# Attention plus retrieved experts on one Trainium2 core: 192 gathered tokens, and the score and value passes run as one behind a lead of 48 blocks

## The chip, the cores and the metric

The kernel runs on one core of a Trainium2 chip. The metric is the device time in microseconds (us), the median of several runs. The core has TensorE (PE: matmuls; its weight loads are shown as PEld), VectorE (DVE), ScalarE (ACT), GpSimd (POOL) and SyncE (SP), which only issues DMAs. Every engine works through its own list of instructions in order and waits on semaphores.

## The reference

One layer of a model: a mixer (sliding-window attention beside an mLSTM), which the change leaves alone, and then a PEER layer of retrieved experts. The second part, for 512 tokens `h` of 1024 numbers, in full precision:

```
q = (ht @ w_q).reshape(T, 8, 2, 128)
s1, s2 = q[:, :, 0] . keys1, q[:, :, 1] . keys2          # 128 keys each
v1, i1 = top_k(s1, 16); v2, i2 = top_k(s2, 16)
top, pos = top_k(v1[..., :, None] + v2[..., None, :], 16)
eidx = (i1 * 128 + i2) at pos                            # 8 x 16 experts of 16384
gate = softmax(top)
act = gelu(u[eidx] . ht) * gate
y = sum over the 128 chosen experts of act * v[eidx]
```

## The kernel before

The 16384 experts lie in 128 blocks of 128 rows of `peer_u` and `peer_v` (1024 numbers each). The first 128 tokens are served by **gathering**: per token and choice one row of `peer_u` is fetched with an indirect DMA (one DMA is a row for each of the 128 tokens, 512 KB), VectorE takes its dot product with the token (L1442), and later the row of `peer_v` is added with its coefficient (L1692); that is 128 gathers of each table. The other 384 tokens are served **densely**: all 128 blocks are multiplied with all these tokens, and a table of gates, zero for experts that a token did not choose, picks out the right ones.

Full precision is had from the reduced-precision matmul format by splitting an operand into a high part (a ScalarE copy) and a low part (VectorE: value minus high part) and adding three products: high by high, high by low, low by high.

Three stages matter here, each a program block of its own that all engines enter and leave together. `query_block` (until about 480 us) makes queries and key scores, and the 16 best of each half. `expert_block` goes over the blocks of `peer_u`: eight transposes turn a block (L1385), ScalarE makes `uH` from PSUM (L1342), VectorE makes `uL` (L1436), 24 matmuls with 384 columns give the scores (L1397, L1400), ScalarE applies Gelu (L1351), and SP stores the result in a table in DRAM. Beside the first 48 of these blocks VectorE ranks the candidates of the four tiles of 128 tokens. Then come 64 blocks that also carry a gate step each: for six tokens VectorE makes two one-hot matrices per token (L1523, L1524), TensorE multiplies them (L1408; one full-precision product is two MATMUL records), and ScalarE copies the 128 x 128 gates of each token into `stage` (L1361), from where SP stores them in DRAM. Sixteen blocks without gates end the stage. `value_block` goes over the blocks of `peer_v`: it loads scores and gates back, VectorE multiplies them into `a` (L1678), both `a` and the block are split (L1651, L1653, L1684, L1687), and 18 matmuls with 512 columns add into six PSUM banks (L1731). Last come the norm (squares at L1661) and the output.

The order is written out by hand: in the lead VectorE's `beside` counts elements worked and puts a `low` where enough have passed.

## Time and profile before

| | |
|---|---|
| median of 3 runs | 1782.9 us (1781.66 to 1788.79) |
| profiled execution, its own time | 1785.9 us |
| its span | 1784.2 us |
| TensorE busy | 94% of the span |
| VectorE, ScalarE busy | 78%, 37% |
| mean granted TensorE clock | 0.968 of full |
| moved by DMA | 426.72 MB |

Busy time is what an engine spent in instructions; matmuls are pipelined, so their durations overlap, and the pace of TensorE is read from starts or from counts of records in a stretch. The span runs from the first to the last instruction; the run's own time is 1.7 us longer.

### The profile page before, as it was taken

Reading aid. Unit: us, or ns where it says so; the run is one execution under the profiler, and the core shown is the slowest. Engines: PE = TensorE matmul, PEld = TensorE weight load, DVE = VectorE, ACT = ScalarE, POOL = GpSimd, SP = SyncE. Lnnn points to the kernel's source line nnn. Section 1 sums busy time; section 2 is a strip of 40 time slices with the busy share of each in tenths; the row PEclk is TensorE's granted clock in tenths of the full one; section 3 lists DMA queues with packets and bytes.
Section 4 is the critical chain, followed back from the end, with each engine's and each line's share of the span. In section 5 each row is a group of like instructions: output and inputs, shape, how many; then the busy total and the mean of one; then the engine's idle time right before and its main releaser. Section 6 shows DMA issues by size and latency. Waiting matters only on the chain. (4 is left out here: it accounts for less than half of the span.)

```text
span 1784.2 us, 26835 instructions
## 1 busy us (share of the span) xinstructions
PE 1670.8 (94%) x8654; PEld 1424.9 (80%) x8654; DVE 1385.7 (78%) x3141; ACT 662.0 (37%) x946; POOL 379.3 (21%) x327
## 2 busy tenths in 40 slices
PE   3999889599699999899999999998999999999996
PEld 2445444378599999899999999997888888888885
DVE  5967556659979997598888888753988888888885
ACT  1102241422144434355555555523333333333332
POOL 1000000034002111132222222221522222232220
PEclk8998999899899999999999999998999999999998
DMA  9562030231146555498888888885999999999981
GB/s 357 181 236 107 1 141 1 58 107 48 60 136 240 187 203 181 146 327 287 303 287 301 290 298 294 298 321 196 407 369 355 354 350 355 356 354 348 359 301 67
DMA packets 178084, 426.72 MB, mean 239 GB/s; under 512 B 14489, under 2 KB 91377, under 8 KB 178033
## 3 DMA queue, kind: packets, MB, share of 16 engines
q1 hardware_dynamic: 131760, 249.68, 39.3%
q0 software_dynamic: 45264, 174.08, 27.9%
q10 hardware_dynamic: 1008, 2.38, 0.4%
q8 instruction: 20, 0.33, 0.1%
q14 instruction: 32, 0.25, 0.0%
HBM read 373.66 MB, written 52.43 MB: 239 GB/s over the span
## 5 line engine op out<-in xcount | busy, mean ns | idle before, releaser
L1397 PE MATMUL S_ps<-hH,uH 128*128 128x384 f32 x1024 | 357.3, 349 | 0.0
L1397 PE MATMUL S_ps<-hL,uH 128*128 128x384 f32 x1024 | 346.3, 338 | 0.0
L1322 POOL DMA_INDIRECT hT<-in_peer_u,eidx x128 | 162.9, 1272 | 543.3 <-DVE dots L1442 475.6
L1651 ACT ACTIVATE vH<-ring 128x1024 fp32r<-128x1024 f32 x128 | 135.8, 1061 | 312.2 <-PE y_ps L1731 309.2
L1731 PE MATMUL y_ps<-vH,aH 128*128 128x512 f32 x768 | 237.7, 391 | 2.1 <-DVE aL L1687 2.1
L1731 PE MATMUL y_ps<-vH,aL 128*128 128x512 f32 x768 | 237.4, 390 | 0.0
L1731 PE MATMUL y_ps<-vL,aH 128*128 128x512 f32 x768 | 237.4, 390 | 0.0
L1436 DVE TENSOR_TENSOR uL<-uT_ps,uH 128x1024 fp32r<-128x1024 f32 x128 | 156.3, 1221 | 101.6 <-ACT uH L1342 97.5
L1684 DVE TENSOR_TENSOR vL<-ring,vH 128x1024 fp32r<-128x1024 f32 x128 | 156.8, 1225 | 85.0 <-ACT vH L1651 85.0
L1621 POOL DMA_INDIRECT hT<-in_peer_v,eidx x128 | 143.6, 1122 | 342.6 <-DVE y L1692 336.4
L1400 PE MATMUL S_ps<-hH,uL 128*128 128x384 f32 x1024 | 201.1, 338 | 2.2 <-DVE uL L1436 2.2
L1397 PEld LDWEIGHTS S_ps<-hL,uH 128*128 128x128 f32 x1024 | 193.2, 189 | 0.0
L1397 PEld LDWEIGHTS S_ps<-hH,uH 128*128 128x128 f32 x1024 | 193.2, 189 | 0.0
L1400 PEld LDWEIGHTS S_ps<-hH,uL 128*128 128x128 f32 x1024 | 182.2, 188 | 2.5 <-DVE uL L1436 2.5
L1731 PEld LDWEIGHTS y_ps<-vH,aH 128*128 128x128 f32 x768 | 144.8, 189 | 32.9 <-DVE aL L1687 2.8
L1731 PEld LDWEIGHTS y_ps<-vL,aH 128*128 128x128 f32 x768 | 144.7, 188 | 30.2
L1731 PEld LDWEIGHTS y_ps<-vH,aL 128*128 128x128 f32 x768 | 144.7, 188 | 30.2
L1351 ACT ACTIVATE act_out<-S_ps 128x384 f32<-128x384 f32 x128 | 62.8, 491 | 282.0 <-PE S_ps L1400 281.6
L1692 DVE SCALAR_TENSOR_TENSOR y<-hT,coef,y 128x1024 f32<-128x1024 f32 x128 | 163.6, 1278 | 0.9 <-DMA hT<-in_peer_v,eidx 0.9
L1442 DVE CUSTOM_DVE_ANT_0 hT<-hT,h_rows 128x1024 f32<-128x1024 f32 x128 | 152.7, 1215 | 2.7 <-DMA hT<-in_peer_u,eidx 2.7
L1385 PE MATMUL uT_ps<-ident,ring 128*128 128x128 f32 x1024 | 135.0, 276 | 15.8 <-DMA ring<-in_peer_u 15.8
L1342 ACT ACTIVATE uH<-uT_ps 128x1024 fp32r<-128x1024 f32 x128 | 133.9, 1046 | 33.0 <-PE uT_ps L1385 32.7
(277 smaller groups left out, 2387.4 us busy)
## 6 DMA issues: line engine op xcount, KB each, us to landing
ring<-in_peer_u SPq DMA_DIRECT2D x128, 512.0 KB, 5.8
ring<-in_peer_v SPq DMA_DIRECT2D x128, 512.0 KB, 5.6
gelu_table<-act_out SPq DMA_DIRECT2D x128, 192.0 KB, 4.2
gate_table<-stage SPq DMA_DIRECT2D x32, 768.0 KB, 7.5
s_in<-gelu_table SPq DMA_DIRECT2D x128, 192.0 KB, 5.5
...
```

What stands on the lines that cost most here:

```text
L1322: pool.indirect_dma_start(u_rows[:, k % RING, :], None, A["peer_u"][0], bass.IndirectOffsetOnAxis(eidx[:, k:k + 1], 0)).then_inc(rows_in[k ...
L1342: func(uH[:, b, :], uT_ps[:, b, :], ACT.Copy).then_inc(u_high, 1)
L1385: last = tr(uT_ps[:, b, c * P:(c + 1) * P], ub[:, r, c * P:(c + 1) * P], ident[:])
L1397: mm(S_ps[:, b, 0:TD], uH[:, b, c * P:(c + 1) * P], h[:, c, P:T], start=(c == 0 and h is hH), stop=False)
L1400: last = mm(S_ps[:, b, 0:TD], uL[:, b, c * P:(c + 1) * P], hH[:, c, P:T], start=False, stop=(c == DC - 1))
L1436: v.tensor_tensor(uL[:, b, :], uT_ps[:, b, :], uH[:, b, :].bitcast(F32), ALU.subtract).then_inc(u_low, 1)
L1442: v.tensor_tensor_reduce(out=u_rows[:, q, :], in0=u_rows[:, q, :], in1=h_rows[:], scale=1.0, scalar=0.0, op0=ALU.mult, op1=ALU.add, accum_ ...
L1621: pool.indirect_dma_start(v_rows[:, k % RING, :], None, A["peer_v"][0], bass.IndirectOffsetOnAxis(eidx[:, k:k + 1], 0)).then_inc(rows_in[k ...
L1651: func(vH[:, q, :], vb[:, q, :], ACT.Copy).then_inc(v_hi, 1)
L1684: v.tensor_tensor(vL[:, q, :], vb[:, q, :], vH[:, q, :].bitcast(F32), ALU.subtract).then_inc(v_lo, 1)
L1692: v.scalar_tensor_tensor(out=y0[:, q % 2, :], in0=v_rows[:, q, :], scalar=coef[:, bass.ds(n, 1)], in1=y0[:, q % 2, :], op0=ALU.mult, op1=A ...
L1731: last = mm(y_ps[:, t, h, :], x[:, q, t * P:(t + 1) * P], w[:, q, h * 512:(h + 1) * 512], start=False, stop=False)
```

## The change

- 192 tokens are gathered instead of 128. The extra 64 need only half a gather's rows per choice, so two choices share one DMA: 64 more gathers of each table, 384 in all. 320 tokens are left for the dense way.
- Six gather buffers instead of four.
- `expert_block` and `value_block` become one `peer_block`. Its first part, the **lead**, has turns 0 to 47: scores of 48 blocks, stored to DRAM, and within them all gate steps (80 steps of four tokens, in turns 19 to 47: 16, 32 and 32 steps for the three token tiles, at one or two, three or four, and four per turn). From turn 48 on each turn does the scores of one block and the values of a block scored two turns before, without DRAM between (80 turns); the 48 lead blocks get their values at the end, in 48 turns and two that drain.
- In the lead the low part is made without VectorE: TensorE adds minus the high part to the block in PSUM (two matmuls, `lead_less`), and ScalarE copies what is left (`lead_low`).
- Of a gate step's one-hot matrices VectorE makes the first of all four tokens in one instruction and the second of two; ScalarE makes the second of the other two, by Abs and Relu (`gate_rows`). The gate product is written to PSUM with a step of four elements, and ScalarE stages four tokens at once (`stage_gates`).
- The ranking works on one tile at a time and hands each on: softmax in `settle` (VectorE), turned by TensorE, copied back in `choice_turned`, at turns 9, 18, 29 and 39.
- In the fused part the block is turned and split in halves. High and low parts of `a` lie interleaved; for the first 64 dense tokens one weight load of both serves, so a value takes 16 matmuls instead of 18, and a fold at the end adds them up. There is one slot for the split value block while scores run, and two after.
- The gather turns are planned ahead: 56 rows in the lead, 284 in the 80 fused turns (three or four each), 44 in 44 of the last ones.
- `query_block` also transposes the 64 extra tokens (eight transposes, two copies).

The core of the diff:

```
-GT = 6
+NA, NB = P, 64
+T0 = NA + NB
+TD = T - T0
+KB = K * NB // P
+GT = 4
-TB = 2 * GT
+TB = 20
-BG = 16
-GP = BG // 4
+BG = 8
+NHOT = 4
+RING = 4
+PE_BLOCK, PE_STEP = 4.8, 0.92
-RING = 4
-TAIL = NBLK - LEAD - GSTEPS
-LOW_EVERY = 2900
-DOTS_LEAD = 20
-DOTS_AFTER = GSTEPS + 8
+SEL_AT = {0: 9, 1: 18, 2: 29, 3: 39}
+ROWS_LEAD, ROWS_TAIL = (40, 16), 44
+NF = NBLK - LEAD
+END = LEAD + 2 + NBLK
+ORDER = list(range(LEAD, NBLK)) + list(range(LEAD))
+TILES = [0, 2, 3, 1]
+RG = 6
+NROWS = 2 * (K + KB)
+STEPS_OF = {1: NB // GT, 2: P // GT, 3: P // GT}
+EIDX_B_AT = RG
...
+def gate_steps():
+    steps, m = [[] for _ in range(LEAD)], 0
+    ends = {1: SEL_AT[2], 2: SEL_AT[3], 3: LEAD - 1}
+    for t in (1, 2, 3):
+        for it, n in spread(STEPS_OF[t], range(SEL_AT[t] + 1, ends[t] + 1)).items():
+            steps[it] = list(range(m, m + n))
+            m += n
+    return steps
...
+                if j == EIDX_B_AT:
+                    pool.wait_ge(eidx_ready, 2)
+                    pool.dma_start(eidx[NB:P, K:K + KB], chosen_u[0:NB, 0, KB:K]).then_inc(eidx_b_in, 16)
...
+            def lead_high(n):
+                act.wait_ge(u_turned, n + 1)
+                if n >= 2:
+                    act.wait_ge(u_done, n - 1)
+                func(H[:, n % 2, :], uT_of(n % 2), ACT.Copy).then_inc(u_high, 1)
+            def lead_low(n):
+                act.wait_ge(u_less, n + 1)
+                func(L[:, n % 2, :], uT_of(n % 2), ACT.Copy).then_inc(u_low, 1)
...
+            def gate_rows(m):
+                b, q = m % NHOT, m % 2
+                act.wait_ge(selT_done, 2 * tile_of(m))
+                if m >= NHOT:
+                    act.wait_ge(g_full, m - NHOT + 1)
+                for k in range(GT - 2, GT):
+                    d = GT * m + k
+                    ins = func(away[:, q, k - GT + 2, :], iota[:], ACT.Abs, bias=negT[:, 0, d:d + 1])
+                ins.then_inc(away_done, 1)
+                act.wait_ge(away_done, m + 1)
+                for k in range(GT - 2, GT):
+                    d = GT * m + k
+                    ins = func(onehot[:, b, k, 1, :], away[:, q, k - GT + 2, :], ACT.Relu, scale=negT[:, 1, d:d + 1], bias=selT[:, 2, d:d + 1])
+                ins.then_inc(hot_act, 1)
+            def stage_gates(m):
+                q, t0 = m // (TB // GT), GT * (m % (TB // GT))
+                act.wait_ge(g_full, m + 1)
+                if t0 == 0 and q >= 2:
+                    act.wait_ge(g_stored[q % 2], 16 * (q // 2))
+                func(stage[:, q % 2, :, t0:t0 + GT], ps[:, 6 + m % 2, :].rearrange("p (i t) -> p i t", t=GT), ACT.Copy).then_inc(g_staged, 1)
...
+            for it in range(LEAD):
+                if it + 1 < LEAD:
+                    lead_high(it + 1)
+                    lead_low(it + 1)
+                gelu(it, 4 + it % 2)
+                for t in range(NT):
+                    if it == SEL_AT[t] - 1:
+                        act.wait_ge(top_ready, t + 1)
+                        func(top[:, t, :, :], top[:, t, :, :], ACT.Exp).then_inc(gate_exp, 1)
+                for m in STEPS[it]:
+                    stage_gates(m)
+                if it + 1 < LEAD:
+                    for m in STEPS[it + 1]:
+                        gate_rows(m)
...
+            for n in range(LEAD, END):
+                w = n - LEAD - 1
+                if LEAD < n <= NBLK:
+                    gelu(n - 1, 6 + (n - 1) % 2)
+                if n < NBLK:
+                    act.wait_ge(half_turned, n - LEAD + 1)
+                    act.wait_ge(u_done, n)
+                    func(H[:, 0, 0:512], ps[:, 6 + n % 2, :], ACT.Copy).then_inc(ua_high, 1)
+                if 0 <= w < NBLK:
+                    act.wait_ge(a_ready, w + 1)
+                    if w >= 2:
+                        act.wait_ge(v_done, w - 1)
+                    func(aHL[:, w % 2, :, 0], a[:, w % 2, :], ACT.Copy).then_inc(a_hi, 1)
+                if n < NBLK:
+                    act.wait_ge(u_turned, n + 1)
+                    func(H[:, 0, 512:D], ps[:, 7 - n % 2, :], ACT.Copy).then_inc(ub_high, 1)
+                if 0 <= w < NBLK:
+                    act.wait_ge(v_in[w % RING], 16 * (w // RING + 1))
+                    wait_slot(act, w)
+                    func(H[:, slot_of(w), :], vb[:, w % RING, :], ACT.Copy).then_inc(v_hi, 1)
...
+            def lead_less(n):
+                pe.wait_ge(u_high, n + 1)
+                for i in range(2):
+                    last = mm(ps[:, 2 * (n % 2) + i, :], minus_one[:], H[:, n % 2, i * 512:(i + 1) * 512],
+                              start=False, stop=True, skip_group_check=True)
+                last.then_inc(u_less, 1)
+            def scores_high(bank, b):
                 for c in range(DC):
                     for h in (hH, hL):
+                        mm(ps[:, bank, 0:TD], H[:, b, c * P:(c + 1) * P], h[:, c, T0:T], start=(c == 0 and h is hH), stop=False)
+            def scores_low(bank, b):
                 for c in range(DC):
+                    last = mm(ps[:, bank, 0:TD], L[:, b, c * P:(c + 1) * P], hH[:, c, T0:T], start=False, stop=(c == DC - 1))
                 last.then_inc(u_done, 1)
...
+            def gates(m):
+                pe.wait_ge(hot_dve, m + 1)
+                pe.wait_ge(hot_act, m + 1)
+                if m >= 2:
+                    pe.wait_ge(g_staged, m - 1)
+                for k in range(GT):
+                    last = mm(ps[:, 6 + m % 2, :].rearrange("p (i t) -> p t i", t=GT)[:, k, :], onehot[:, m % NHOT, k, 0, :],
+                              onehot[:, m % NHOT, k, 1, :], start=True, stop=True)
+                last.then_inc(g_full, 1)
...
+            for it in range(LEAD):
+                if it + 1 < LEAD:
+                    lead_turn(it + 1)
+                pe.wait_ge(u_high, it + 1)
+                if it >= 2:
+                    pe.wait_ge(s_ready, it - 1)
+                scores_high(4 + it % 2, it % 2)
+                if it + 1 < LEAD:
+                    lead_less(it + 1)
+                pe.wait_ge(u_low, it + 1)
+                scores_low(4 + it % 2, it % 2)
+                for m in STEPS[it]:
+                    gates(m)
...
+            def value(w, part):
+                s, b, first, final = slot_of(w), w % 2, w == 0, w == NBLK - 1
+                aH, aL = aHL[:, b, :, 0], aHL[:, b, :, 1]
+                both = aHL[:, b, 0:NB, :].rearrange("p t i -> p (t i)")
+                if part == 0:
+                    pe.wait_ge(v_hi, w + 1)
...
+                            mm(y_bank(g, h), aH[:, NB + g * P:NB + (g + 1) * P], H[:, s, h * 512:(h + 1) * 512], start=first, stop=False)
+                else:
...
+                    pe.wait_ge(v_lo, w + 1)
+                    for g in range(2):
+                        for h in range(2):
+                            mm(y_bank(g, h), aH[:, NB + g * P:NB + (g + 1) * P], L[:, s, h * 512:(h + 1) * 512], start=False, stop=final)
+                    for h in range(2):
+                        last = mm(y_bank(2, h), both, L[:, s, h * 512:(h + 1) * 512], start=False, stop=final)
+                    last.then_inc(v_done, 1)
...
+            for n in range(LEAD, END):
+                w = n - LEAD - 2
...
+                if n < NBLK:
+                    pe.wait_ge(u_in[n % RING], 16 * (n // RING + 1))
+                    turn(n, 0)
+                if w >= 0:
+                    value(w, 0)
+                if n < NBLK:
+                    if n > LEAD:
+                        pe.wait_ge(s_ready, n)
+                    turn(n, 1)
+                if w >= 0:
+                    value(w, 1)
+                if n < NBLK:
+                    pe.wait_ge(ua_high, n - LEAD + 1)
+                    pe.wait_ge(ub_high, n - LEAD + 1)
+                    pe.wait_ge(ua_low, n - LEAD + 1)
+                    scores_high(6 + n % 2, 0)
+                    pe.wait_ge(ub_low, n - LEAD + 1)
+                    scores_low(6 + n % 2, 0)
...
+            def hot_rows(m):
+                b, d0 = m % NHOT, GT * m
+                if m >= NHOT:
+                    dve.wait_ge(g_full, m - NHOT + 1)
+                v.tensor_tensor(onehot[:, b, :, 0, :], iota[:].unsqueeze(1).broadcast_to([P, GT, P]),
+                                selT[:, 0, d0:d0 + GT].unsqueeze(2).broadcast_to([P, GT, P]), ALU.is_equal)
+                for k in range(GT - 2):
+                    d = d0 + k
+                    ins = v.tensor_scalar(onehot[:, b, k, 1, :], iota[:], selT[:, 1, d:d + 1], selT[:, 2, d:d + 1], ALU.is_equal, ALU.mult)
+                ins.then_inc(hot_dve, 1)
+            clock, due, blk = 0.0, 0.0, 0
...
+            for n in range(LEAD, END):
+                w = n - LEAD - 1
+                left = ROWS_AT[n]
+                if n < NBLK:
+                    dve.wait_ge(ua_high, n - LEAD + 1)
+                    v.tensor_tensor(L[:, 0, 0:512], ps[:, 6 + n % 2, :], H[:, 0, 0:512].bitcast(F32), ALU.subtract).then_inc(ua_low, 1)
+                if 0 <= w < NBLK:
+                    if w < NF:
+                        dve.wait_ge(s_ready, LEAD + w + 1)
+                        src = act_out[:, (LEAD + w) % 2, :]
+                    else:
+                        dve.wait_ge(s_loaded[w % RING], 16 * ((w - NF) // RING + 1))
+                        src = s_in[:, w % RING, :]
+                    g = (w // BG) % 2
+                    dve.wait_ge(g_in[g], 16 * (w // (2 * BG) + 1))
+                    if w >= 2:
+                        dve.wait_ge(a_hi, w - 1)
+                    v.tensor_tensor(a[:, w % 2, :].rearrange("p (q t) -> p q t", t=TB), src.rearrange("p (q t) -> p q t", t=TB),
+                                    gbuf[:, g, :, w % BG, :], ALU.mult).then_inc(a_ready, 1)
+                if n < NBLK and left > 3:
+                    take_row()
+                    left -= 1
+                if n < NBLK:
+                    dve.wait_ge(ub_high, n - LEAD + 1)
+                    v.tensor_tensor(L[:, 0, 512:D], ps[:, 7 - n % 2, :], H[:, 0, 512:D].bitcast(F32), ALU.subtract).then_inc(ub_low, 1)
+                if left > 1:
+                    take_row()
+                    left -= 1
+                if 0 <= w < NBLK:
+                    dve.wait_ge(a_hi, w + 1)
+                    v.tensor_tensor(aHL[:, w % 2, :, 1], a[:, w % 2, :], aHL[:, w % 2, :, 0].bitcast(F32), ALU.subtract).then_inc(a_lo, 1)
+                if left > 1:
+                    take_row()
+                    left -= 1
+                if 0 <= w < NBLK:
+                    dve.wait_ge(v_hi, w + 1)
+                    s = slot_of(w)
+                    v.tensor_tensor(L[:, s, :], vb[:, w % RING, :], H[:, s, :].bitcast(F32), ALU.subtract).then_inc(v_lo, 1)
+                for _ in range(left):
+                    take_row()
+            assert rows_taken == NROWS
```

## Rows read from the trace of the kernel before

**Rows 1.** The page, part 1: busy us, share, instructions.
```profile
PE 1670.8 (94%) x8654; PEld 1424.9 (80%) x8654; DVE 1385.7 (78%) x3141; ACT 662.0 (37%) x946; POOL 379.3 (21%) x327
```

**Rows 2.** Stretches: us, busy per engine (x records), granted clock, DMA share, GB/s.
```profile
500.00:700.00 200.00, 200.00 (x1260) 198.72 (x1258) 177.40 (x374) 84.31 (x100) 33.46 (x20) 1.00 0.57 192
800.00:1100.00 300.00, 300.00 (x2051) 300.00 (x2050) 266.32 (x744) 164.85 (x208) 82.34 (x70) 1.00 0.86 296
1300.00:1700.00 400.00, 400.00 (x1766) 331.22 (x1766) 329.29 (x393) 144.39 (x196) 114.31 (x122) 1.00 0.96 354
1244.00:1260.00 16.00, 16.00 (x66) 13.03 (x65) 16.00 (x21) 7.60 (x10) 12.39 (x7) 0.90 1.03 403
718.00:740.00 22.00, 17.59 (x100) 16.80 (x99) 8.94 (x22) 6.79 (x9) 0.00 (x0) 0.84 0.38 122
```

**Rows 3.** Timeline of PE: first turn; one lead block.
```profile
481.84 3.68 PE L1385 MATMUL uT_ps<-ident,ring 128*128 128x128 f32 x16 [15.84 <-DMA ring<-in_peer_u]
...
562.45 0.34 PE L1397 MATMUL S_ps<-hH,uH 128*128 128x384 f32 x1
...
564.73 0.34 PE L1397 MATMUL S_ps<-hL,uH 128*128 128x384 f32 x1
```

**Rows 4.** Groups of ScalarE: busy us, mean ns of one.
```profile
L1651 ACT ACTIVATE vH<-ring 128x1024 fp32r<-128x1024 f32 x128 | 135.8, 1061 | 312.2 <-PE y_ps L1731 309.2 <-PEq L1718 2.8 <-DMA ring<-in_peer_v 0.2
...
L1342 ACT ACTIVATE uH<-uT_ps 128x1024 fp32r<-128x1024 f32 x128 | 133.9, 1046 | 33.0 <-PE uT_ps L1385 32.7
...
L1361 ACT ACTIVATE stage<-G_ps 128x384 f32<-128x384 f32 x128 | 101.1, 898 | 39.4 <-PE G_ps L1408 39.4
...
L1653 ACT ACTIVATE aH<-a 128x384 fp32r<-128x384 f32 x128 | 65.0, 508 | 16.9 <-DVE a L1678 16.9
L1351 ACT ACTIVATE act_out<-S_ps 128x384 f32<-128x384 f32 x128 | 62.8, 491 | 282.0 <-PE S_ps L1400 281.6
...
L1351 ACT ACT_TABLE_LOAD x28 | 35.9, 1283 | 43.9 <-PE S_ps L1400 43.9
...
L1134 ACT ACTIVATE peer_qT<-query_psum 128x512 f32<-128x512 f32 x16 | 9.6, 598 | 73.3 <-PE query_psum L1180 73.3
```

**Rows 5.** Timeline of ScalarE: small activations with a bias column.
```profile
257.84 0.39 ACT L651 ACTIVATE decay<-x_sb,gcol 128x128 f32<-128x128 f32 x1
258.13 0.39 ACT L649 ACTIVATE decay<-x_sb,gcol 128x128 f32<-128x128 f32 x1
```

**Rows 6.** Groups of VectorE: busy us, mean ns of one.
```profile
L1692 DVE SCALAR_TENSOR_TENSOR y<-hT,coef,y 128x1024 f32<-128x1024 f32 x128 | 163.6, 1278 | 0.9 <-DMA hT<-in_peer_v,eidx 0.9
...
L1442 DVE CUSTOM_DVE_ANT_0 hT<-hT,h_rows 128x1024 f32<-128x1024 f32 x128 | 152.7, 1215 | 2.7 <-DMA hT<-in_peer_u,eidx 2.7
...
L1523 DVE TENSOR_SCALAR onehot<-iota,selT 128x128 f32<-128x128 f32 x384 | 110.4, 288 | 22.6 <-PE G_ps L1408 20.3
```

**Rows 7.** Timeline of VectorE: one value block.
```profile
1400.62 1.23 DVE L1684 TENSOR_TENSOR vL<-ring,vH 128x1024 fp32r<-128x1024 f32 x1 [0.72 <-ACT vH L1651]
1401.77 0.55 DVE L1687 TENSOR_TENSOR aL<-a,aH 128x384 fp32r<-128x384 f32 x1
1402.23 1.28 DVE L1692 SCALAR_TENSOR_TENSOR y<-hT,coef,y 128x1024 f32<-128x1024 f32 x1
1403.43 0.55 DVE L1678 TENSOR_TENSOR a<-s_in,s_all 128x384 f32<-128x384 f32 x1
```

**Rows 8.** VectorE from 479 to 701: all, L1436, L1442; one wait.
```profile
479.00:701.00 222.00, 196.12 (x462) 0.98 0.57 192
...
479.00:701.00 222.00, 52.62 (x43) 0.98 0.57 192
...
479.00:701.00 222.00, 19.57 (x32) 0.98 0.57 192
...
DVE uL L1436 <- ACT uH L1342: 20.2, 14, 3.5
```

**Rows 9.** The chain in order of time: start, us, what.
```profile
1241.52 525.17 PE y_ps L1731 x2304
```

732 lines of the change are left out of this document (339 added, 393 removed).

## The prediction

> **What bounds the kernel now.** I read the page's busy times first [rows 1]: TensorE is at 94%, VectorE at 78%, ScalarE at 37%. An average says little over stages, so the stretches came next [rows 2]. From 500 to 1700 TensorE is busy throughout but for two gaps, at full clock. Records give its pace. Lead: 32 per block, 1260 in 200 us, 5.08 us a block. Gate blocks: 44 per block, 2051 in 300 us, 6.44 us. Value blocks: 525.17 us for 128 [rows 9], 4.10 us. The reader is to see that VectorE, at 89% beside the first two and 82% in the third, is close behind, and that DMA moves 354 GB/s in the values at a share of 0.96. So fewer TensorE columns pay one for one, as long as the other engines keep up at the new pace.
>
> **Unit prices.** 384-column matmuls start 0.1754 us apart (13 steps from 562.45 to 564.73 [rows 3]); 24 take 4.21 of the 5.08, which leaves 0.87 for eight transposes. 512 columns: 400 us for 1766 [rows 2], 0.2265. The line through both gives 0.150 for 320 columns, an estimate. One one-hot product: (6.44 - 5.08)/6 = 0.226. VectorE, start to start [rows 7]: split of 1024 1.15, of 384 0.46, row added 1.20; so 0.60 for 512 and 0.39 for 320. A dot is 1.215 long and starts about 0.07 early on the next, 1.145 [rows 6]. ScalarE [rows 4]: 1024 long 1.05, 512 from PSUM 0.60, 384 0.49; a small one with a bias column 0.39 long, the next 0.30 later [rows 5]; a table load 1.28.
>
> **Part by part.**
>
> Query stage: eight more transposes and two copies, +1.5. TensorE begins the lead at 481.8 [rows 3], then at 483.3.
>
> Lead on TensorE alone: a block is 24 x 0.150 + 0.87 + 2 x 0.2265 = 4.92; a gate step 4 x 0.226 = 0.90. 48 x 4.92 + 80 x 0.90 = 308, so it could end at 791. VectorE does not stop it in total: the ranking cost it 222 - 43 splits x 1.15 - 16 dots x 1.145 - 20 of waiting [rows 8] = 134; 80 gate steps at 0.59 + 2 x 0.26 = 1.1 (the one-hot of 512 elements by the 512 price, the other two by L1523) are 88; 56 dots 64; hand-overs 8: 294.
>
> ScalarE does. Its order in a turn is: high part of the next block, low part, Gelu, staging of this turn's gates, one-hots for the next turn. A step's one-hots are two Abs, a wait for their own result, two Relu: 0.30 + 0.39 + 0.05 + 0.30 + 0.30, about 1.3. Nothing of this overlaps TensorE's half of the loop: `lead_less` of the next block needs the high part, which stands behind the one-hots; these stand behind the staging of the last gate; that stands behind the scores' low products. Queued behind ScalarE's wait are the Gelu, the stores and the next Abs. The loop with k steps now and k' next is 1.2 (low products) + 0.9k + 0.8 (last result, staging) + 1.3k' + 1.0 (high) + 0.65 (two matmuls and their result) = 3.65 + 0.9k + 1.3k'. At k = 3 that is 10.3 against 7.6 of TensorE, at k = 4 12.5 against 8.5. Turns 0 to 18 have no steps: 19 x 4.92, 3 for two switches to Exp and back (two loads and 0.3 each, partly covered), 1.5 for the slow first turn: 98. Turns 19 to 29: 11 x 3.65 + 16 x 2.2 = 75, and about 10 for the first hand-over (Exp, `settle`, transposes, copy, one-hots, gates, each after the other): 85. Turns 30 to 47: 18 x 3.65 + 64 x 2.2 = 206, and 5 for the hand-over at 39: 211. Lead 394, ending at 877. Bounds: if the Abs and Relu were hidden, the lead is TensorE's 308 and the 20 of hand-overs, switches and slow start, ending at 811, 66 less; with staging at the 0.90 of L1361, whose writes are strided as these are in part, +12 to +25. I take contiguous runs of four as free.
>
> Staging and gate product: the product goes to PSUM with a step of four elements. No row shows such a write. The line above makes 0.0004 us of a column, 0.051 of 128 columns, and the records of L1408 stand 0.113 apart (0.226 for two), so over half of each is slack for the write. I take nothing; four times the time would add 0.9 a step, 72.
> The Trainium skill (SBUF — State Buffer, Door 1: The DMA port swizzle) says that any non-contiguous access to PSUM slows matmuls significantly. By that rule the sum would be some 70 higher; by the row it is not.
>
> Hand-over to the fused part: scores of turns 48 and 49 need no values, 2 x 4.47 + 1 = 10. The first `a` waits for the last gate store, then two gate groups of 1.3 MB, behind four value blocks; 4.7 MB with the store at 403 GB/s [rows 2] and some 4 of latency is 16 after the lead's end, where VectorE blocks at 7. The stall is 9, and 1 more for the clock: a stop of 9.5 cost 0.84 over 22 before [rows 2]. +10.
>
> Fused turns, 78: 3.60 + 0.87 + 16 x 0.2265 = 8.09, 631. VectorE: two halves 1.2, `a` and its low part 0.78, value split 1.15, 3.55 rows x 1.15 to 1.20: 7.2 to 7.4, below 8.09. ScalarE 3.2. The single value slot is free at 4.5 of a turn, high part to 5.6, low part to 7.0, needed at 9.9 of the same count: hidden. DMA: 0.52 for each block, 0.16 of gates, 3.55 x 0.52 of rows = 3.07 MB a turn, 380 GB/s. Before, 403 GB/s ran for 16 us [rows 2], so 7.6 us a turn: hidden, with 6% to spare. I add 4.
>
> Last 50 turns: TensorE needs 16 x 0.2265 = 3.62. But VectorE does `a`, its low part, the value split, then the row; ScalarE makes the value's high part only after the high part of `a`. With `a` of the next turn behind the row on VectorE this closes a loop: split 1.15, row 1.20, `a` 0.48 + 0.03, ScalarE 0.38 to its next, value high 1.06 + 0.03 [rows 4, 7] = 4.33. 44 x 4.33 + 6 x 3.62 = 212, 31 more than TensorE's own.
>
> End: before 17.5 from the last value matmul (1766.7 to 1784.2). Six closing matmuls go (1.4), two copies and two more squares come (2.5): 18.6.
>
> Sum: 877 + 10 + 10 + 631 + 212 + 18.6 + 4 = 1762.6 of span, against 1784.2: 21.6 less. The profiled run was 3 above the median, so the forecast is 1782.9 - 22 = 1761 us. Of some 147 us that the cut in TensorE's work would give, 86 go to ScalarE's loop and hand-overs in the lead, 31 to the loop at the end.
>
> **The rivals.**
> A, the lead is TensorE's and VectorE's: ScalarE's one-hots hide. For it: ScalarE is at 37%, and in a turn of k = 4 it is busy only 9.5 us. Against: the order above. Then 877 becomes 811: 1695.
> Where the Abs and Relu stand in one table set with Gelu they cost no load, which no row shows; the Trainium skill (ScalarE: Activation LUTs, Table sets: the hidden batching unit) says that every set has both.
> B, the other side: DMA bounds the fused turns. For it: 354 GB/s at a share of 0.96 [rows 2] may be the ceiling, not the demand; then a turn is 3.07/0.354 = 8.68 and the gathers, whose buffers come free as VectorE takes rows, come late: +47 less the 4, 1804. It makes the kernel slower from 31 us on, a turn of 8.5, that is a rate under 362 GB/s. Against: 403 GB/s with both queues full.
> C, the strided gate products: +72, 1833. Against: the slack above.
> D, the end runs at TensorE's pace, 3.62: -31, 1730. Then ScalarE gets `a` early enough.
> E, the stops of 3 to 4 us in each late lead turn let the clock fall; half of TensorE's 5 us in the loop doubled over 18 turns is +45, 1806. From 800 on before, TensorE never stopped, so no row excludes it.
>
> **How the numbers follow.** Chances: forecast 0.40 (own range 1735 to 1790), A 0.20, B 0.16, C 0.06, D 0.08, E 0.10. 1761 is the forecast's own time. From 1690, which takes in A, to 1815, which takes in B and E, all but C and the far ends stand: 0.8. Half a per cent is 9 us, about what a measurement can tell: faster is under 1774, slower over 1792. Faster: A, D, and 0.28 of the forecast, 0.56. Slower: B, C, E less 0.06, and 0.02, 0.28. Same 0.16.
>
> **What would show it.** Lead: L1385 to the end of the gate products 394 us; ScalarE's high part of the late turns waits for nothing but its own one-hots, and `lead_less` waits 3 to 4 us for it in each of turns 30 to 47; granted clock 1.00. VectorE some 100 us idle there. Fused: 8.1 us a turn, rows never late by DMA. End: 4.3 us a turn, ScalarE waiting for `a`. It would be wrong if ScalarE's small activations overlap more than 0.30 apart, if gathers land later than 9 us, or if the gate records are longer than 0.113 apart.

## The result and the profile after

The changed kernel takes 1812.6 us (median of four runs, 1810.1 to 1814.1) beside 1784.5 for the kernel before on the same chip: ratio 1.014, 95% interval 1.013 to 1.016. It is slower by 1.4%, and the interval lies clear of 1. The forecast was 1761. The profiled execution has a span of 1808.2, where the working summed to 1762.6, so 45.6 us are to be found.

The page's busy times of the changed kernel, to be read against [rows 1]: TensorE has 73 us less to do, and yet the span is 24 longer.

```profile
PE 1598.1 (88%) x8370; PEld 1331.0 (74%) x8370; DVE 1384.5 (77%) x2859; ACT 725.2 (40%) x1307; POOL 500.1 (28%) x424
```

Its stretches, with the columns of [rows 2] (busy time per engine, granted clock, DMA share, GB/s):

```profile
500.00:700.00 200.00, 174.65 (x1197) 167.69 (x1196) 174.35 (x461) 130.95 (x221) 51.35 (x37) 0.97 0.69 225
700.00:800.00 100.00, 75.75 (x443) 72.23 (x442) 37.67 (x89) 68.05 (x142) 12.25 (x10) 0.79 0.51 160
800.00:900.00 100.00, 68.70 (x423) 65.49 (x423) 48.82 (x114) 70.79 (x156) 18.35 (x14) 0.84 0.60 187
900.00:1000.00 100.00, 80.86 (x468) 74.90 (x469) 64.33 (x111) 36.87 (x69) 34.91 (x30) 0.87 0.87 314
1000.00:1500.00 500.00, 500.00 (x2959) 457.17 (x2959) 457.47 (x637) 188.88 (x309) 251.88 (x220) 1.00 0.99 380
1600.00:1700.00 100.00, 93.34 (x380) 71.38 (x380) 76.56 (x93) 33.24 (x47) 19.85 (x21) 1.00 0.92 318
```

The reader is to see three kinds of stretch. From 1000 to 1500, the fused part, TensorE never stops and its clock is 1.00. From 1600 on it stops for 7% of the time, at full clock. From 700 to 900 no engine is full: TensorE 76 and 69%, VectorE 38 and 49%, ScalarE 68 and 71%. That is what a loop of hand-overs looks like; and there the granted clock is 0.79 and 0.84. A busy share is also higher at half clock, because the same work takes longer.

One late lead turn of four gate steps, ScalarE's timeline (start, duration, line, out<-in, count, idle time before and what ended it):

```profile
817.60 0.69 ACT L1462 ACTIVATE s_all<-iota,negT 128x128 f32<-128x128 f32 x2
818.32 0.88 ACT L1467 ACTIVATE s_all<-s_all,selT,negT 128x128 f32<-128x128 f32 x2
819.11 0.68 ACT L1462 ACTIVATE s_all<-iota,negT 128x128 f32<-128x128 f32 x2
...
822.83 0.88 ACT L1467 ACTIVATE s_all<-s_all,selT,negT 128x128 f32<-128x128 f32 x2
823.62 1.00 ACT L1438 ACTIVATE hi_slots<-peer_psum 128x1024 fp32r<-128x1024 f32 x1
825.93 1.02 ACT L1443 ACTIVATE lo_slots<-peer_psum 128x1024 fp32r<-128x1024 f32 x1 [1.31 <-PE peer_psum L1550]
828.03 0.44 ACT L1451 ACTIVATE s_all<-peer_psum 128x320 f32<-128x320 f32 x1 [1.07 <-PE peer_psum L1561]
828.92 0.60 ACT L1475 ACTIVATE stage<-peer_psum 128x512 f32<-128x512 f32 x1 [0.45 <-PE peer_psum L1570]
...
831.72 0.60 ACT L1475 ACTIVATE stage<-peer_psum 128x512 f32<-128x512 f32 x1 [0.30 <-PE peer_psum L1570]
832.22 0.69 ACT L1462 ACTIVATE s_all<-iota,negT 128x128 f32<-128x128 f32 x2
```

The same turn on TensorE (the sixteen high products, L1557, start at 817.9 and are left out):

```profile
816.91 1.04 PE L1542 MATMUL peer_psum<-ident,ring 128*128 128x128 f32 x8
824.67 1.22 PE L1550 MATMUL peer_psum<-hi_slots,minus_one 128*128 128x512 f32 x2 [4.38 <-ACT hi_slots L1438]
825.69 2.30 PE L1561 MATMUL peer_psum<-hH,lo_slots 128*128 128x320 f32 x8
827.83 3.86 PE L1570 MATMUL peer_psum<-s_all 128*128 128x128 f32 x32
```

Read the two together, from 817.60 to the same point at 832.22, 14.6 us. ScalarE makes four steps' one-hots (6.0 us, 1.51 each), then the high part. TensorE had its transposes at 817 and its high products by 820.3, and stops 4.38 us. When it goes on it is at half clock: two `lead_less` products take 1.22, eight low products 2.30 (1.34 at full clock, below). ScalarE waits for each of them in turn, stages four gates, and starts again. While ScalarE finishes its one-hots and the high part TensorE has nothing to do. Behind that the two answer each other, and only the first stagings run beside gate products.

Turns, from the start of one Gelu to the next: up to 18 mostly 4.86 us each, 19 to 29 7.7 on average (84.3 in all). In turns 30 to 47 those of three steps take 11.3 to 13.4 and those of four 15.2 on average; they alternate between about 14.8 and 15.7, because in every second one part of the gate products is at the lower clock too (32 of them take 5.03 us from 842.43, for 3.86 above). The last gate products end at 919.9, and the transposes of turn 48 start at 920.6.

The hand-over after the lead, VectorE's first `a` and TensorE's first high products after it, from the timeline:

```profile
927.13 0.80 SPq L1363 DMA_DIRECT2D stage<-gate_table  x2
...
940.66 0.49 DVE L1841 TENSOR_TENSOR s_all<-s_all,stage 128x320 f32<-128x320 f32 x1 [12.36 <-DMA stage<-gate_table]
...
941.58 0.57 ACT L1510 ACTIVATE hi_slots<-peer_psum 128x512 fp32r<-128x512 f32 x1
```

```profile
942.25 0.61 PE L1557 MATMUL peer_psum<-hH,hi_slots 128*128 128x320 f32 x1 [14.56 <-ACT hi_slots L1510]
942.65 0.47 PE L1557 MATMUL peer_psum<-hL,hi_slots 128*128 128x320 f32 x1
942.92 0.47 PE L1557 MATMUL peer_psum<-hH,hi_slots 128*128 128x320 f32 x1
```

Products of 320 columns start 0.27 us apart here; in an early lead turn at full clock it is 0.146. The engine had stopped for 14.56 us, and this pace, 1.8 times slower, is that of the lower of the two clock levels, 1.2 of 2.4 GHz. The regular fused turns then run from 948.1, 8.12 us each. The waits of the whole execution (total, times, longest):

```profile
ACT a_hi_lo L1507 <- DVE s_all L1841: 190.5, 85, 13.6
...
DVE s_all L1734 <- PE peer_psum L1570: 110.0, 17, 8.8
...
PE peer_psum L1550 <- ACT hi_slots L1438: 76.4, 25, 4.8
...
ACT lo_slots L1443 <- PE peer_psum L1550: 56.0, 44, 3.1
```

The largest waits of ScalarE and VectorE are not the loss: VectorE's 110 us are idle time beside the loop. The row that counts is the third, TensorE's 76.4 us in 25 stops: from turn 30 on there are 17, of 2.9 to 4.8 us each.

### The profile page after: what moved, and what is told of

Its sections match the earlier page's. It is cut to its first block, busy times and chain, and to the rows that moved or that the text cites. A ratio compares the mean times of both kernels' runs of the same rounds, so it can differ in the third digit from the quotient of the medians.

```text
span 1808.2 us, 23463 instructions
## 1 busy us (share of the span) xinstructions
PE 1598.1 (88%) x8370; PEld 1331.0 (74%) x8370; DVE 1384.5 (77%) x2859; ACT 725.2 (40%) x1307; POOL 500.1 (28%) x424
## 4 chain that ended last, share of the span: by engine, by line
PE 47%; ACT 10%; DVE 8%; issue 7%; DMA 1%; another core or an unknown queue 0%; SPq 0%; DVEq 0%; ACTq 0%
PE peer_psum L1557 12%; PE peer_psum L1561 8%; PE peer_psum L1570 5%; PE peer_psum L1618 4%; PE peer_psum L1629 4%; PE peer_psum L1625 4%; PE peer_psum L1605 4%; DVE s_all L1706 3%; ACT hi_slots L1514 3%; ACT s_all L1462 3%; ACT s_all L1467 2%; PE peer_psum L1622 2%; PE peer_psum L1631 2%; PE peer_psum L1550 2%; ACT hi_slots L1438 1%
## 5 line engine op out<-in xcount | busy, mean ns | idle before, releaser
L1557 PE MATMUL peer_psum<-hH,hi_slots 128*128 128x320 f32 x1024 | 309.0, 315 | 15.6 <-ACT hi_slots L1510 14.6
L1557 PE MATMUL peer_psum<-hL,hi_slots 128*128 128x320 f32 x1024 | 304.6, 311 | 0.0
L1557 PEld LDWEIGHTS peer_psum<-hH,hi_slots 128*128 128x128 f32 x1024 | 194.7, 190 | 19.5 <-issue 14.8
L1557 PEld LDWEIGHTS peer_psum<-hL,hi_slots 128*128 128x128 f32 x1024 | 194.8, 190 | 3.0
L1561 PE MATMUL peer_psum<-hH,lo_slots 128*128 128x320 f32 x1024 | 187.1, 329 | 0.0
L1561 PEld LDWEIGHTS peer_psum<-hH,lo_slots 128*128 128x128 f32 x1024 | 173.4, 206 | 5.6
L1861 DVE TENSOR_TENSOR lo_slots<-s_all,hi_slots 128x1024 fp32r<-128x1024 f32 x128 | 156.6, 1224 | 21.7 <-ACT hi_slots L1514 21.7
L1618 PE MATMUL peer_psum<-hi_slots,a_hi_lo 128*128 128x512 f32 x512 | 151.4, 417 | 12.3 <-ACT hi_slots L1514 12.3
L1706 DVE SCALAR_TENSOR_TENSOR s_all<-hT,coef,s_all 128x1024 f32<-128x1024 f32 x126 | 161.3, 1280 | 1.0 <-DMA hT<-in_peer_v,eidx 0.9
L1625 PE MATMUL peer_psum<-hi_slots,a_hi_lo 128*128 128x512 f32 x512 | 139.3, 393 | 0.0
L1618 PEld LDWEIGHTS peer_psum<-hi_slots,a_hi_lo 128*128 128x128 f32 x512 | 90.5, 195 | 39.7 <-ACT hi_slots L1514 29.1
L1625 PEld LDWEIGHTS peer_psum<-hi_slots,a_hi_lo 128*128 128x128 f32 x512 | 99.2, 194 | 20.1
L1550 PE MATMUL peer_psum<-hi_slots,minus_one 128*128 128x512 f32 x96 | 40.7, 512 | 76.4 <-ACT hi_slots L1438 76.4
## 6 DMA issues: line engine op xcount, KB each, us to landing
slab<-in_w_mod SPq DMA_DIRECT2D x5, 2048.0 KB, 15.2
```

The costliest lines, as they stand in the source:

```text
L1550: last = mm(ps[:, 2 * (n % 2) + i, :], minus_one[:], H[:, n % 2, i * 512:(i + 1) * 512], start=False, stop=True, skip_group_check=True)
L1557: mm(ps[:, bank, 0:TD], H[:, b, c * P:(c + 1) * P], h[:, c, T0:T], start=(c == 0 and h is hH), stop=False)
L1561: last = mm(ps[:, bank, 0:TD], L[:, b, c * P:(c + 1) * P], hH[:, c, T0:T], start=False, stop=(c == DC - 1))
L1618: mm(y_bank(g, h), aH[:, NB + g * P:NB + (g + 1) * P], H[:, s, h * 512:(h + 1) * 512], start=first, stop=False)
L1625: mm(y_bank(g, h), aL[:, NB + g * P:NB + (g + 1) * P], H[:, s, h * 512:(h + 1) * 512], start=False, stop=False)
L1706: v.scalar_tensor_tensor(out=y0[:, i, :], in0=rows_of(j), scalar=c, in1=y0[:, i, :], op0=ALU.mult, op1=ALU.add).then_inc(row_done, 1)
```

## The experiments

All are edits of the changed kernel. The ratio is to the kernel before on the same chip; 0.01 is 18 us, and the changed kernel's ratio is 1.0143. "Lead" runs from the first transposes to the Gelu of turn 48 in the profiled execution. (The first transposes start anywhere from 476.5 to 485.4 us in these executions, so ends of stretches can't be compared as they stand.) The last column is a lead turn of four steps, the commonest value of turns 41 to 46 or, where they alternate, their mean.

| kernel | median us | ratio, 95% interval | lead us | four steps |
|---|---|---|---|---|
| changed | 1812.6 | 1.0143 (1.0126 to 1.0160) | 448.8 | 15.2 |
| e1_rows_after_high | 1767.2 | 0.9881 (0.9842 to 0.9920) | 401.4 | 13.45 |
| e2_onehots_on_vector | 1722.7 | 0.9633 (0.9597 to 0.9670) | 353.8 | 8.80 |
| e3_clock_kept | 1785.1 | 0.9979 (0.9958 to 1.0000) | 419.3 | 13.18 |
| e4_row_before_low | 1790.0 | 1.0007 (0.9980 to 1.0033) | 442.1 | 15.2 |
| e5_low_by_vector | 1860.8 | 1.0414 (1.0389 to 1.0438) | 496.5 | 16.0 |
| e6_gates_first | 1801.6 | 1.0067 (1.0046 to 1.0089) | 445.4 | 15.2 |
| e7_three_edits | 1692.1 | 0.9468 (0.9444 to 0.9491) | 352.3 | 8.80 |
| e8_planner_price | 1686.0 | 0.9441 (0.9416 to 0.9465) | 347.1 | 8.80 |
| e9_low_behind_rows | 1773.7 | 0.9909 (0.9874 to 0.9945) | 411.3 | 10.5 |
| e10_two_and_two | 1752.4 | 0.9808 (0.9770 to 0.9845) | 389.1 | 11.33 |
| e11_shared_one_hots | 1690.3 | 0.9446 (0.9415 to 0.9477) | 347.6 | 8.80 |

### e1_rows_after_high: the order on ScalarE

```
                 if it + 1 < LEAD:
                     lead_high(it + 1)
+                for m in STEPS[it]:
+                    gate_rows(m)
+                if it + 1 < LEAD:
                     lead_low(it + 1)
...
                     stage_gates(m)
-                if it + 1 < LEAD:
-                    for m in STEPS[it + 1]:
-                        gate_rows(m)
```

> ScalarE's one-hots of a turn are made behind the high part of the next block instead of ahead of it; the work is the same. Loop theory (the high part stands behind the one-hots, and TensorE can do nothing without it): a turn of four steps falls from 15.2 us to ScalarE's own 1.05 + 4 x 1.51 + 1.0 + 0.4 + 1.6 = 10.1 us or a little over, TensorE's stop before `lead_less` goes, and the granted clock stays near 1.00; the lead ends some 80 us sooner, 1725 to 1740 us. Rival, VectorE or the hand-overs set the late turns: no change, within 9 us of 1812. Rival, ScalarE's amount of work and not its order sets the pace: under 20 us saved.

1767 us: 47 less by the ratios, where 72 to 87 were expected. TensorE's stop before `lead_less` is gone, and turns of three steps take 9.4 us. But four steps take 13.45, not 10.1 (the mean of turns 41 to 46 is 12.9), and the clock is 0.95 from 700 to 770 and 0.90 from 770 to 870, not near 1.00. Order is what matters, so both rivals fall; but half of the saving at four steps is missing. TensorE's timeline of this kernel says why:

```profile
812.78 3.04 PE L1570 MATMUL peer_psum<-s_all 128*128 128x128 f32 x16 [3.13 <-ACT stage L1475]
...
819.50 0.62 PE L1550 MATMUL peer_psum<-hi_slots,minus_one 128*128 128x512 f32 x2
819.96 1.34 PE L1561 MATMUL peer_psum<-hH,lo_slots 128*128 128x320 f32 x8
```

The stop has moved to the third gate product: the products have two banks, and ScalarE stages the first only behind all its one-hots, the low part and the Gelu. e10 tests that.

### e10_two_and_two: give the banks back earlier

The edit is shown against e1.

```
                 if it + 1 < LEAD:
                     lead_high(it + 1)
-                for m in STEPS[it]:
+                for m in STEPS[it][:2]:
                     gate_rows(m)
...
+                todo = list(STEPS[it])
+                for i, m in enumerate(STEPS[it][2:]):
+                    gate_rows(m)
+                    for _ in range(2 if i == 0 else 1):
+                        stage_gates(todo.pop(0))
+                for m in todo:
+                    stage_gates(m)
```

> As e1_rows_after_high, but ScalarE makes only the first two steps' one-hots ahead of the low part; those of the third and fourth step alternate with the stagings. Theory for what e1 left (13.45 us at four steps, where ScalarE is busy 10.1): the third gate product needs one of the two gate banks, which ScalarE gives back only behind all its one-hots, the low part and the Gelu, and the next block's transposes stand behind the products. With the banks given back between the one-hots: 11.2 to 12 us at four steps, 9.4 at three as in e1, 10 to 18 us less: 1750 to 1757. Rival, it is something else (the low clock, the one-hots of VectorE): within 5 us of 1767.

1752 us, as expected, 13 under e1 by the ratios. Of turns 41 to 46 three take 11.33, and the others 12.7 to 13.0; the mean is 12.1 for e1's 12.9. TensorE's stop at the third gate product falls from 3.1 to 1.65, with one of 0.80 at the fourth, and from 800 to 857, ahead of the hand-over, the clock is still 0.91. So the bank was a part of e1's rest and not all of it.

### e2_onehots_on_vector: ScalarE's part moved away

```
-                for k in range(GT - 2):
+                for k in range(GT):
                     d = d0 + k
                     ins = v.tensor_scalar(onehot[:, b, k, 1, :], ...)
...
-                pe.wait_ge(hot_act, m + 1)
```
and `gate_rows` is not called.

> All four second one-hots of a step are made by VectorE with its compare-and-multiply; ScalarE's Abs and Relu go. VectorE gets 80 x 2 x 0.26 = 42 us more in the lead. Loop theory: a late turn is TensorE's 8.5 us or VectorE's 8.7; the lead ends about 100 us sooner, 1705 to 1725 us. Rival, VectorE is as close to the bound as ScalarE, because of the ranking: 1750 or more. If the clock's fall had another cause than the stops, it would still show 0.8 from 700 on here.

1722.7 us, inside what was expected: 91 less than the changed kernel. A turn of four steps is 8.80, one of three 7.65. The stretch from 700 to 800, beside the changed kernel's 75.75 and 0.79:

```profile
700.00:800.00 100.00, 97.79 (x740) 95.21 (x738) 91.04 (x253) 56.84 (x81) 23.66 (x19) 1.00 0.88 293
```

TensorE is full and at full clock; VectorE, with 42 us more to do, is at 91%. VectorE takes 0.26 us for the one-hot that costs ScalarE 0.75 (half of 1.51), and it stood idle there. Its timeline in this kernel, the four second one-hots of a step (the next instruction starts at 778.09):

```profile
777.06 1.11 DVE L1734 TENSOR_SCALAR s_all<-iota,selT 128x128 f32<-128x128 f32 x4
```

So the work stood on the wrong engine for this stage of the loop: ScalarE was the less busy engine on the page, and the one that everything waited for.

### e3_clock_kept: what the clock alone costs

```
                 scores_high(4 + it % 2, it % 2)
+                if len(STEPS[it]) >= 3:
+                    for i in range(24):
+                        mm(ps[:, 4 + it % 2, 0:TD], zeros[:], hH[:, i % DC, T0:T], start=False, stop=False)
```

`zeros` is a matrix of zeros, made once, so the products add nothing.

> The order of the lead stays; in turns with three or more gate steps TensorE does 24 more 320-column products with a zero matrix (adding nothing) where it stops, 3.6 us. Theory that the stops cost twice, once as a wait and once by the clock: granted clock 0.95 or more from 700 to 930, `lead_less` and the low products at 0.6 and 1.3 us instead of 1.2 and 2.3, a late turn of 13.3 to 13.7 us, 25 to 35 us less: 1778 to 1787. Rival, the clock costs nothing here because ScalarE alone sets the loop: within 9 us of 1812. Rival, the clock falls for a reason other than the stops: clock as before and the 24 products lengthen nothing or up to 40 us.

More work, and 29 us less by the ratios; the lead is 29.5 shorter. Two rows of stretches and TensorE's timeline of a late turn:

```profile
700.00:800.00 100.00, 94.79 (x693) 92.55 (x692) 44.90 (x107) 78.06 (x163) 14.84 (x12) 1.00 0.58 184
800.00:900.00 100.00, 93.14 (x674) 90.27 (x673) 52.59 (x120) 75.89 (x165) 20.55 (x16) 0.98 0.72 226
```

```profile
823.72 0.72 PE L1552 MATMUL peer_psum<-hi_slots,minus_one 128*128 128x512 f32 x2 [0.85 <-ACT hi_slots L1439]
824.28 1.33 PE L1563 MATMUL peer_psum<-hH,lo_slots 128*128 128x320 f32 x8
```

`lead_less` takes 0.72 for 1.22 and the low products 1.33 for 2.30. The gate products take 3.85 in every turn, where the changed kernel has 3.9 to 4.1 and 5.0 to 5.2 by turns. A turn of four steps is 13.18 and one of three 11.17. That is the loop at full clock. The forecast's formula gives 12.5 and 10.3, and with 1.51 instead of 1.3 for a step's one-hots 13.3 and 10.9.

### e4_row_before_low: the last 50 turns

```
-                if n < NBLK and left > 3:
+                if left > (3 if n < NBLK else 0):
                     take_row()
                     left -= 1
```

> In the last 50 turns VectorE takes its row between `a` and the low part of `a`, not behind the value's low part; the work is the same. Theory of the loop at the end (`a` of the next turn stands behind the row, ScalarE's high value part behind the high part of `a`): the loop shortens by the 1.20 of a row to under TensorE's 3.62, the last 50 turns fall from 208 to 182 to 188 us, 1786 to 1793 in all. Rival, the value blocks' DMA or the wait for the free slot sets the 4.25 us: no change. Rival, TensorE then waits for the low part of `a`, which is now 1.2 late: under 8 us saved.

1790.0 us, 24 less by the ratios, as expected. VectorE's timeline of the changed kernel in this part:

```profile
1660.82 1.28 DVE L1706 SCALAR_TENSOR_TENSOR s_all<-hT,coef,s_all 128x1024 f32<-128x1024 f32 x1
1662.01 0.48 DVE L1841 TENSOR_TENSOR s_all<-s_in,stage 128x320 f32<-128x320 f32 x1
1663.06 0.49 DVE L1854 TENSOR_TENSOR a_hi_lo<-s_all,a_hi_lo 128x320 fp32r<-128x320 f32 x1 [0.56 <-ACT a_hi_lo L1507]
1663.99 1.23 DVE L1861 TENSOR_TENSOR lo_slots<-s_all,hi_slots 128x1024 fp32r<-128x1024 f32 x1 [0.44 <-ACT hi_slots L1514]
```

and of e4:

```profile
1663.14 0.48 DVE L1841 TENSOR_TENSOR s_all<-s_in,stage 128x320 f32<-128x320 f32 x1
1663.54 1.28 DVE L1706 SCALAR_TENSOR_TENSOR s_all<-more_rows,coef,s_all 128x1024 f32<-128x1024 f32 x1
1664.78 0.49 DVE L1854 TENSOR_TENSOR a_hi_lo<-s_all,a_hi_lo 128x320 fp32r<-128x320 f32 x1
```

In the changed kernel VectorE stands idle twice in a turn, each time for ScalarE's answer. With the row put into the first of these gaps the gap is filled, `a` comes sooner, the turn falls from 4.32 to 3.72 us and TensorE is full (100 of the 100 us from 1600 on). The same instructions in another order save 0.6 us a turn.

### e5_low_by_vector and e9_low_behind_rows: the low parts back on VectorE

In both, `lead_less` and ScalarE's `lead_low` are gone, and VectorE subtracts:

```
+            def lead_low(n):
+                dve.wait_ge(u_high, n + 1)
+                if n >= 2:
+                    dve.wait_ge(u_done, n - 1)
+                v.tensor_tensor(L[:, n % 2, :], uT_of(n % 2), H[:, n % 2, :].bitcast(F32), ALU.subtract).then_inc(u_low, 1)
```

> The lead's low parts go back to VectorE, which subtracts the high part from the block in PSUM; TensorE's two products with minus one and ScalarE's copy of the rest go, everything else stays as changed. Loop theory: the high part of the next block is then wanted a turn later, so ScalarE's one-hots are out of the loop and only its own work counts: at four steps 4 x 1.51 + 1.03 + 0.42 + 4 x 0.54 = 9.7 us a turn instead of 15.2. VectorE gets 48 x 1.15 = 55 us more in the lead, at most 350 of the 437. The lead ends 60 to 80 us sooner: 1732 to 1752 us, granted clock 0.95 or more from 700 on. Rival, the low parts were rightly taken off VectorE (the ranking leaves it no room): the turns up to 30 get as much longer as the later ones get shorter, 1790 or more.

1860.8 us, 48 above the changed kernel, where 60 to 80 less were expected. VectorE's timeline (and TensorE's gate products after it):

```profile
851.56 1.22 DVE L1742 TENSOR_TENSOR lo_slots<-peer_psum,hi_slots 128x1024 fp32r<-128x1024 f32 x1 [7.07 <-ACT hi_slots L1438]
852.70 0.68 DVE L1729 TENSOR_TENSOR s_all<-iota,selT 128x512 f32<-128x512 f32 x1
...
853.95 5.47 PE L1568 MATMUL peer_psum<-s_all 128*128 128x128 f32 x32 [6.00 <-DVE s_all L1733]
```

The low part was put ahead of VectorE's own one-hots of the turn. It waits 7.07 us for ScalarE's high part, which stands behind ScalarE's one-hots; VectorE's one-hots stand behind that wait, and TensorE's gates behind those. The loop was not opened, it was led over one engine more. In e9 the low part stands behind VectorE's one-hots:

> As e5_low_by_vector, but VectorE makes the low part of the next block behind its one-hots of the turn, not ahead of them. In e5 the low part waited for ScalarE's high part, which stands behind ScalarE's one-hots, and VectorE's one-hots stood behind that wait: the loop had only moved to VectorE (16 us a turn). Theory that this queue was all of e5's late loss: a turn of four steps falls from 16 to 10.5 to 12 us, VectorE's wait of 7 us before the low part ends no longer ahead of the gates; with turns 0 to 18 at some 6 us as in e5 (VectorE is full there) the lead ends 80 to 100 us sooner than e5's, 1760 to 1785 us, that is 30 to 50 under the changed kernel. Rival, VectorE's low part is late by itself: still 14 us or more a turn, 1830 or more.

1773.7 us, as expected; four steps take 10.5 us in three of turns 41 to 46 and 11.0 to 12.0 in the others, and VectorE's wait is 2.5:

```profile
877.56 1.22 DVE L1742 TENSOR_TENSOR lo_slots<-peer_psum,hi_slots 128x1024 fp32r<-128x1024 f32 x1 [2.53 <-ACT hi_slots L1438]
```

Both kernels pay in the early turns, where VectorE still ranks: turns 1 to 18 take 6.2 and 6.3 us on average against 5.0. From the first transposes to the Gelu of turn 29 e5 takes 219.6 us and e9 217.8, the changed kernel 186.5: the rival of e5's expectation holds there, and it is 33 of the 48 us. In turns 30 to 47 e5 takes 265.7, e9 183.8 and the changed kernel 251.0: there the place in the queue decides. So with the one-hots shared as they are, each of the two places for the low part is the better one in one part of the lead: TensorE and ScalarE while VectorE ranks, VectorE once ScalarE makes one-hots. No run combines them.

### e6_gates_first: the hand-over to the fused part

```
-            for w in range(RING):
-                load_v(w)
             for i in range(2):
                 sp.wait_ge(g_stored[i], 16 * (NTB // 2))
-            for i in range(2):
-                load_g(i)
+            load_g(0)
+            for w in range(RING):
+                load_v(w)
+                if w == 1:
+                    load_g(1)
```

> Between lead and fused part SyncE loads the first group of gates ahead of the value blocks and the second behind two of them, not both behind four. Theory that the first `a` waits for 4.7 MB of which it needs 1.3: its wait on the gates falls from 12.4 us to 3 to 6, the stop of TensorE from 14.6 to 6 to 8, 1803 to 1807 us. Rival, the time is the store of the last gates and a DMA's latency, not what stands ahead: no change, 1812.

1801.6 us, 14 less by the ratios, a little more than the 6 to 10 expected. Waits of e6 from 780 to 960 us:

```profile
PE peer_psum L1558 <- ACT hi_slots L1511: 7.7, 1, 7.7
DVE s_all L1842 <- DMA stage<-gate_table: 5.5, 1, 5.5
```

The wait on the gates falls from 12.4 to 5.5 and TensorE's stop from 14.6 to 7.7, as expected. The turn that holds it, 21.8 us from Gelu to Gelu in the changed kernel, takes 15.0. The traces show these 7 us; the other 7 are not explained, and the intervals of the two ratios leave some 5 us either way.

### e7, e8 and e11: together, and two finer shares

> e2_onehots_on_vector (all one-hots on VectorE), e4_row_before_low (tail) and e6_gates_first (order of loads) together. If the three losses lie in different stages they add: 1722.7 - 22 - 8 = 1693 us, from 1688 to 1700. If e4's saving depended on the pace before it, or the transition's on the DMA traffic, 1700 to 1715.

1692.1 us, as expected. The single savings, 91, 24 and 14, sum to 129; together they give 121 by the ratios. They are losses of different stages and nearly add.

e8 changes one number of e7, `clock += 1.15` to `clock += 1.67`.

> e7 with one number more: the price that VectorE's planner sets for a step's one-hots is 1.67 us instead of 1.15, as they now take that long, so that it changes over from the ranking to lead blocks less late. Theory that the uneven turns 22 to 30 (7.6 to 11.5 us) come from this: 3 to 8 us less than e7. Rival, VectorE is simply full there: within 3 us of e7.

1686.0 us: 6 less in the medians and 5 in the lead (347.1 for 352.3), and in the traces the gain lies where the planner acts: turns 19 to 29 take 81.1 us for 86.7. The intervals of the two ratios overlap, so the direction fits and the size is not settled. Its stretches:

```profile
500.00:700.00 200.00, 184.50 (x1303) 176.52 (x1303) 192.04 (x520) 103.80 (x133) 54.25 (x38) 1.00 0.71 235
700.00:800.00 100.00, 97.23 (x733) 94.18 (x731) 95.34 (x266) 55.85 (x80) 23.95 (x19) 1.00 0.87 288
```

e11 leaves two of the four second one-hots of the first 16 steps on ScalarE (`for k in range(GT - 2 if m < STEPS_OF[1] else GT)`, and `gate_rows` for these steps alone).

> As e8_planner_price, but the first 16 gate steps (turns 19 to 29, beside VectorE's last ranking) keep the changed kernel's split, two second one-hots on VectorE and two on ScalarE; the other 64 steps are VectorE's alone. VectorE has 16 x 0.52 = 8 us less there, where it is full (8.6 us a turn in e8, 7.1 in the changed kernel). Theory that each engine should have them where it has room: 5 to 12 us under e8, 1674 to 1681. Rival, ScalarE's loop costs as much there as VectorE's load: within 4 us of 1686, or above.

1690.3 us: nothing is gained, as the rival said. The lead is 347.6 for 347.1. Turns 20 to 28 take 62.5 us for e8's 65.7, but turn 19, the first hand-over, takes 11.65 for 7.72: ScalarE's one-hots stand in its chain again. By the ratios e8 (0.9441) and e11 (0.9446) can't be told apart: both are some 5.5% under the kernel before.

## Why the prediction was wrong

The step that failed is the term of turns 30 to 47, and the larger part of it is the clock: it was set against the forecast as a case of its own (rival E), when it comes on top of the forecast's loop. With the clock kept up the kernel would still hardly have been faster than before (e3: ratio 0.998, where the forecast is 0.988), so the smaller parts share in the miss. By the prediction's own steps, in us of span:

| step | forecast | measured | what the runs say |
|---|---|---|---|
| start of the lead | 483.3 | 477.8 | 5.5 earlier, cause open |
| turns 0 to 18 | 98 | 102.2 | +4, 2 of it one long turn |
| turns 19 to 29 | 85 | 84.3 | right |
| turns 30 to 47 | 211 | 251.0 | +40: clock and the price of a one-hot |
| last Gelu of the lead to turn 48 | 0 | 5.3 | +5, the last gate products |
| turns 48, 49 and the stall | 20 | 27.5 | +8, stall longer |
| fused turns, 78, with DMA | 635 | 633 | right, 8.12 each for 8.09 |
| last 50 turns | 212 | 208 | -4 |
| end | 18.6 | 18.9 | right |

From the first transposes to the end of the gate products the lead takes 442 us, where the forecast had 394.

**ScalarE's loop in the lead** is the mechanism, and the forecast had it in order and in place: `lead_less` waiting behind the high part behind the one-hots. e1, e2, e9 and e10 open it at different links, and each saves 42 to 91 us; e3 shows its pace at full clock. Rival A, that the one-hots hide, is refuted.

**The price of a step's one-hots** was mis-sized: 1.3 forecast, 1.51 measured. The forecast took 0.30 from start to start from [rows 5], an activation with a bias column alone. The Relu has two, a scale and a bias: in the page's groups it is 489 ns long beside the Abs's 391, and the timeline has 0.79 from the first Relu of a pair to the next Abs, 0.72 from the first Abs to the first Relu (groups: busy us, mean ns of one):

```profile
L1467 ACT ACTIVATE s_all<-s_all,selT,negT 128x128 f32<-128x128 f32 x160 | 70.6, 489 | 2.7
...
L1462 ACT ACTIVATE s_all<-iota,negT 128x128 f32<-128x128 f32 x160 | 54.7, 391 | 10.0 <-DVE negT L1727 10.0
```

Then 0.2 x 64 steps is 13 us in turns 30 to 47. The Trainium skill (ScalarE: Activation LUTs, What ACT_TABLE_LOAD costs) says that each column operand adds some 93 ns, which this trace bears out (391 to 489).

**The clock** is the larger part, 29 us: e3 fills the stops with work that adds nothing and gets the lead 29.5 shorter, all of it in turns 30 to 47 (221.4 for 251.0). With the 13 for the price that is 42.5 for the 40 missing, so the rest of the loop is 2 to 3 us shorter than forecast. The forecast had priced the clock at +45 with a chance of 0.10 and as another world, 1806 in all; the loop of 3 to 4 us stops that it did forecast was the condition for it. "No row excludes it" is true, but a row speaks for it, and it was misread: the 0.84 from 718 to 740 [rows 2] stands with a stop of TensorE of 4.4 us and not of 9.5. The 9.5 are VectorE's wait in the same stretch. From the kernel before:

```profile
732.18 0.69 DVE L1507 TENSOR_REDUCE tsum<-top 128x32 f32<-128x512 f32 x1 [9.51 <-ACT top L1367]
```

```profile
PE G_ps L1420 <- DVE top L1509: 4.4, 1, 4.4
```

From 734 to 740, behind that stop, the granted clock was 0.62, and from 740 on 1.00 again. That is a stop as long as those forecast for each late lead turn, so the one measured case was on hand. What speaks to it in the Trainium skill (TensorE: Matmul & The Clock Gate, What's actually happening) is that half rate is the default and activity lifts it; the trace agrees: 0.79 and 0.84 where TensorE stops 2.9 to 4.8 us in each turn, 1.00 and 0.98 in the same stretches of e3, where its longest stop is 1.3.

**The hand-over** was right in kind and short by 8: VectorE's stall came to 12.4 instead of 9, TensorE's stop was 14.6, and it restarted at half clock (0.27 apart for sixteen products). e6 shows that the order of the loads was 7 us of it: the same stop is 13.3 to 17.9 us in e1, e2, e3 and e10, which leave that order.

**The fused turns**: rival B falls. The DMA moved 380 GB/s at a share of 0.99 while TensorE was never idle, so 354 at 0.96 [rows 2] was the demand and not the ceiling.

**The strided gate products**: rival C falls. They start 0.112 us apart at the median (32 take 3.86 us, 0.12 each with the waits in it), beside 0.113 before. The Trainium skill's rule (SBUF — State Buffer, Door 1: The DMA port swizzle) that a non-contiguous access to PSUM slows matmuls significantly is not seen here, for 128 columns written four elements apart; no run here shows other steps or widths.

**The end**: rival D falls; 4.32 us a turn with a row, as forecast (4.33). e4 shows the named loop to be the cause: with the row elsewhere it is 3.72.

Of what the forecast said would show it, the 110 us of VectorE's idle time, the stop before `lead_less` and ScalarE's wait for `a` were there; the granted clock of 1.00 was not. All rows but two came within 6 us, and the sum still had the wrong sign, because its margin, 21.6 us of 1784, was smaller than the two effects on one term. Stops and clock should have been one case: a forecast of stops of 3 to 4 us in 18 successive turns has the slower engine after each stop in it, or says why not.

Two slips changed nothing. The price of VectorE's second one-hot, 0.26, was put down to L1523, which has one operation; the one with two is L1524, and it starts 0.26 from the next as well. And the cut in TensorE's work is worth 152 us by the working's own terms, not 147.

What stays open: why the lead starts at 476 to 485 us from one execution to the next, how large e8's gain over e7 is, and what keeps three of e10's late turns 1.3 to 1.7 us longer than the others.
